# A hybrid encoder trunk on one core: the input projection with 512-column products, its halves added on eviction, a reordered opening, and short rows padded to 128

## The reference, cut to what matters

```python
u = rmsnorm(h, norm_mix[l])
proj = u @ w_in[l]
p_mla, p_ssm, p_swa = jnp.split(proj, [MLA_COLS, MLA_COLS + SSM_COLS], axis=-1)
y_a = mla_mixer(p_mla, cos, sin, ...)      # 6 heads, 128 + 64 rotary features
y_b = mamba2_mixer(p_ssm, ...)             # conv of 4 taps, SiLU, SSD scan, 12 heads
y_c = swa_mixer(p_swa, sinks, ...)         # 8 heads of 64, 2 key heads
h = h + jnp.concatenate([y_a, y_b, y_c], axis=-1) @ w_out[l]
h = h + cross_attention(rmsnorm(h, norm_cross[l]), rmsnorm(mem, norm_mem[l]), ...)
h = h + conv_ffn(rmsnorm(h, norm_ffn[l]), ...)
return rmsnorm(h, norm_final)

def causal_dwconv(x, w, b):                # in mamba2_mixer: k_w = 4
    xp = jnp.pad(x, ((0, 0), (k_w - 1, 0), (0, 0)))
    return sum(xp[:, k:k + seq] * w[k] for k in range(k_w)) + b
```

## Time and profile before

| | |
|---|---|
| median of 3 runs | 1200.29 us (1200.27 to 1201.62) |
| the profiled execution | 1203.7 us, of it 1201.8 us span |
| TensorE busy | 1180.1 us, 98% |
| VectorE busy | 893.1 us, 74% |
| ScalarE busy | 656.4 us, 55% |
| mean granted clock of TensorE | 0.994 |
| HBM | 214.33 MB read, 180 GB/s over the span |

### The profile page before, as it was taken

How to read it: one execution, slowest core, us unless ns; L and a number is a source line. 1 busy time by engine, 2 the same in 40 slices (tenths; PEclk the granted TensorE clock), 3 DMA queues, 4 the chain that set the end, 5 groups by cost and what they waited for, 6 DMA issues and landing times.

```text
span 1201.8 us, 18802 instructions
## 1 busy us (share of the span) xinstructions
PE 1180.1 (98%) x6956; PEld 1040.3 (87%) x6956; DVE 893.1 (74%) x1263; ACT 656.4 (55%) x867; POOL 0.2 (0%) x4
## 2 busy tenths in 40 slices
PE   9899999999999999999999999999999999999996
PEld 8799999988887978888888888888888888888885
DVE  5775998778776667867777777778777777777777
ACT  5545674475654557546464545455464545555454
POOL 0000000000000000000000000000000000000000
PEclk9999999999999999999999999999999999999998
DMA  9666756433566445776666657575767667585751
GB/s 351 197 165 164 194 146 176 131 107 106 188 215 185 148 142 142 222 198 191 192 177 195 188 172 209 175 209 180 204 180 204 175 185 199 172 212 175 210 175 71
DMA packets 303214, 217.11 MB, mean 181 GB/s; under 512 B 11350, under 2 KB 263998, under 8 KB 302526
## 3 DMA queue, kind: packets, MB, share of 16 engines
q1 hardware_dynamic: 302990, 216.31, 61.3%
q10 hardware_dynamic: 176, 0.14, 0.1%
HBM read 214.33 MB, written 2.10 MB: 180 GB/s over the span
## 4 chain that ended last, share of the span: by engine, by line
PE 93%; DVE 3%; ACT 2%; issue 1%; DMA 1%; SPq 0%; ACTq 0%; DVEq 0%
PE bank L1359 27%; PE bank L1363 14%; PE bank L1333 10%; PE bank L1335 10%; PE bank L1334 10%; PE bank L1336 6%; PE bank L1337 6%; PE bank L1338 6%; PE bank L1434 1%; DVE lo L780 1%; ACT hi L386 1%; PE bank L1465 1%; DMA arena<-in_mem_dram 1%; PE bank L1395 1%; PE bank L1385 0%
## 5 line engine op out<-in xcount | busy, mean ns | idle before, releaser
L780 DVE TENSOR_TENSOR lo<-raw,hi 128x2048 fp32r<-128x2048 f32 x195 | 446.5, 2290 | 126.0 <-ACT hi L386 118.4
L386 ACT CAST hi<-raw 128x2048 fp32r<-128x2048 f32 x195 | 371.8, 1912 | 99.7 <-PE bank L1335 98.6
L1359 PE MATMUL bank<-ux,hi 128*128 128x512 f32 x1408 | 336.5, 391 | 0.0
L1359 PEld LDWEIGHTS bank<-ux,hi 128*128 128x128 f32 x1408 | 259.2, 188 | 50.6 <-DVE arena L1261 0.2
L1363 PEld LDWEIGHTS bank<-ux,lo 128*128 128x128 f32 x1408 | 180.9, 191 | 7.1
L1363 PE MATMUL bank<-ux,lo 128*128 128x256 f32 x1408 | 183.1, 283 | 0.0
L1333 PE MATMUL bank<-hi,ch 128*128 128x512 f32 x464 | 181.4, 391 | 1.4 <-DVE cl L1200 1.4
L1334 PE MATMUL bank<-lo,ch 128*128 128x512 f32 x464 | 180.3, 389 | 0.0
L1335 PE MATMUL bank<-hi,cl 128*128 128x512 f32 x464 | 180.2, 388 | 0.0
L1336 PE MATMUL bank<-ux,hi 128*128 128x256 f32 (+1 forms) x592 | 171.0, 289 | 1.2 <-DVE lo L780 1.2
L1337 PE MATMUL bank<-ux,hi 128*128 128x256 f32 (+1 forms) x592 | 167.8, 283 | 0.0
(11 more groups left out here) (241 smaller groups left out, 972.8 us busy)
## 6 DMA issues: line engine op xcount, KB each, us to landing
raw<-in_ffn_w_up_dram SPq DMA_DIRECT2D x88, 1024.0 KB, 5.8
raw<-in_ffn_w_down_dram SPq DMA_DIRECT2D x44, 1024.0 KB, 5.1
raw<-in_w_in_dram SPq DMA_DIRECT2D x28, 1024.0 KB, 5.6
raw<-in_w_out_dram SPq DMA_DIRECT2D x16, 1024.0 KB, 5.2
raw<-in_cross_wkv_dram SPq DMA_DIRECT2D x7, 1024.0 KB, 9.6
arena<-in_x_dram SPq DMA_DIRECT2D x4, 1024.0 KB, 8.5
raw<-in_cross_wq_dram SPq DMA_DIRECT2D x4, 1024.0 KB, 5.4
raw<-in_cross_wo_dram SPq DMA_DIRECT2D x4, 1024.0 KB, 5.1
```

The costliest lines, as they stand in the source:

```text
L386: a.mark(act.copy(hi[:, n % RING, :], raw[:, n % RING, :]), S("hi_ready"))
L780: d.mark(dve.tensor_tensor(lo[:, n % RING, :], raw[:, n % RING, :], hi[:, n % RING, :].bitcast(F32), ALU.subtract), S("lo_ready"))
L1359: pe.matmul(bank[b][:, :], hi[:, s, k * P:(k + 1) * P], ux[:, k, :, :].rearrange("p a b -> p (a b)"), start=(k == 0), stop=False)
```

## The change

1. All 28 full tiles of w_in (8 to 13, 15 to 33 without the latent ones, 38 to 40) use `wide_product`. Its optional `mid` (other heads' work) comes between the two groups of 16. Tile 14 stays as it was.
2. Each such tile is evicted in two steps: ScalarE copies the right half of the bank to the destination (`take_low`), VectorE adds the left half to it (`sum_halves`, signal `tile_summed`). `tile_summed` frees the bank. `summed(n)` counts these signals.
3. In the convolution stage ScalarE does `conv_first(n - 1)`, `conv_low(n)`, `conv_silu(n - 1)` in turn n, and VectorE `sum_halves(n - 1)`, `split(n + 2)`, extras, `conv_rest(n - 1)`.
4. The key tile is copied into four zero-padded tiles, one for each key head and half of the partitions; the rotary key gets a second padded tile `krT_odd`; `pick`, `acum_h` and `acum_l` get 128 rows, of which 116 are zero. The clears and one copy are on VectorE, at tiles 21, 22 and 24.
5. In the opening block 2 moves ahead of the second pair of memory groups, and block 4 ahead of the squares of x.
6. In the end ScalarE scales the first two blocks of t = 0 before its squares of (1, 2), and VectorE scales the other two behind its last add. Two signals go.

The diff, with some context left out:

```diff
--- before.py
+++ after.py
@@
         yT = at(7168, 6, T)
-        swa_q, swa_k, swa_v, swa_kswap = at(8704, 4, T), at(9728, T), at(9984, T), at(10240, T)
+        swa_q, swa_v = at(8704, 4, T), at(9984, T)
+        swa_key = ((at(9728, T), at(12800, T)), (at(10240, T), at(13056, T)))
+        krT_odd = at(19968, T)
+        key_tile = at(4096, T)
         sq_swa = at(8704, 4 * T)
@@
         stat = sb("stat", [P, 2, 8])
-        pick = sb("pick", [SSM_H, SSM_H], F32R)
-        acum_h = sb("acum_h", [SSM_H, T], F32R)
-        acum_l = sb("acum_l", [SSM_H, T], F32R)
+        pick = sb("pick", [P, SSM_H], F32R)
+        acum_h = sb("acum_h", [P, T], F32R)
+        acum_l = sb("acum_l", [P, T], F32R)
         mem_r = sb("mem_r", [P, TT])
@@
                 for half in range(2):
-                    if t == 1 and half == 1:
-                        sp.wait_ge(S("out_ready_act").sem, 2)
+                    if half == t:
+                        sp.wait_ge(S("out_ready_act").sem, 2 * t + 2)
                     else:
-                        sp.wait_ge(S(f"out_ready{t}").sem, 2 * half + 2)
+                        sp.wait_ge(S(f"out_ready{t}").sem, 2)
                     cols = slice(half * 1024, (half + 1) * 1024)
@@
                                       accum_out=parts[:, t, cb:cb + 1]), S(f"final_parts{t}"))
+            def act_scale(t, cbs):
+                act.wait_ge(S("final_r").sem, t + 1)
+                act.wait_ge(S("gained").sem, 4 * t + cbs[-1] + 1)
+                for cb in cbs:
+                    c = slice(cb * 512, (cb + 1) * 512)
+                    a.mark(act.activation(hwork[:, t, c], hwork[:, t, c], ACT.Copy, scale=small[:, s_r + t:s_r + t + 1]), S("out_ready_act"))
@@
+            def take_low(n, b, dst):
+                wait_product(n)
+                a.mark(act.copy(dst, bank[b][:, T:2 * T]), S("low_taken"))
             act.dma_start(tab[:, 0:2 * P], table[:, 0:2 * P]).then_inc(S("consts_landed").sem, 16)
@@
             a.mark(act.copy(hi[:, 0, CH // 2:], raw[:, 0, CH // 2:]), S("hi_ready"))
-            for q in (1, 2, 3):
-                for g in (2 * q, 2 * q + 1):
-                    token_hi("mem", g, V_MEM, mem_bank(g))
-                split(q)
-                if q == 2:
-                    act.wait_ge(S("mem_landed3").sem, 16)
-                    a.mark(act.activation(junk, mems[:, 0, :], ACT.Square, accum_out=small[:, s_ss:s_ss + 1]), S("mem_ss"))
-                    token_root("mem")
+            for g in (2, 3):
+                token_hi("mem", g, V_MEM, mem_bank(g))
+            split(1)
+            split(2)
+            for g in (4, 5):
+                token_hi("mem", g, V_MEM, mem_bank(g))
+            act.wait_ge(S("mem_landed3").sem, 16)
+            a.mark(act.activation(junk, mems[:, 0, :], ACT.Square, accum_out=small[:, s_ss:s_ss + 1]), S("mem_ss"))
+            token_root("mem")
+            for g in (6, 7):
+                token_hi("mem", g, V_MEM, mem_bank(g))
+            split(3)
+            split(4)
             act.wait_ge(S("x_landed").sem, 32)
...
             a.mark(act.activation(xs[:, 0, :], xs[:, 0, :], ACT.Copy, scale=small[:, s_r:s_r + 1]), S("x_scaled"))
-            split(4)
             act.wait_ge(S("vecs_turned").sem, 2)
...
@@
             a.mark(act.copy(dt_rows[0:SSM_H, 0, :], b[64:64 + SSM_H, 0:T]), S("tile_taken"))
+            act.wait_ge(S("tile_summed").sem, summed(N_CQ + 5))
             squares("cq", cq_raw[:, 0:4, :], sq_cq, 4)
...
-            def conv_first(n):
+            def conv_low(n):
...
                 c = n - N_XBC
-                wait_product(n)
                 if c >= RING:
                     act.wait_ge(S("xbc_ready").sem, c - RING + 1)
-                a.mark(act.activation(convacc[:, n % RING, :], bank[n % 3][:, 0:T], ACT.Identity,
+                take_low(n, n % 3, convraw[:, n % RING, :])
+            def conv_first(n):
+                c = n - N_XBC
+                act.wait_ge(S("tile_summed").sem, summed(n))
+                a.mark(act.activation(convacc[:, n % RING, :], convraw[:, n % RING, :], ACT.Identity,
                                       scale=vecs[:, V_CW + 30 + c:V_CW + 31 + c], bias=vecs[:, V_CB + c:V_CB + c + 1]), S("conv_first"))
-                a.mark(act.copy(convraw[:, n % RING, :], bank[n % 3][:, 0:T]), S("tile_taken"))
@@
                     take_x_tok(n - 22)
-                conv_first(n)
+                if n > N_XBC:
+                    conv_first(n - 1)
+                conv_low(n)
                 if n > N_XBC:
...
                 if n == N_QKV:
+                    conv_first(n - 1)
                     conv_silu(n - 1)
@@
                 if k == 4:
-                    wait_product(n)
-                    a.mark(act.copy(swa_kswap[0:64, :], bank[n % 3][64:128, 0:T]), S("kr_parts"))
-                    a.mark(act.copy(swa_kswap[64:128, :], bank[n % 3][0:64, 0:T]), S("kr_parts"))
-                take(n, n % 3, swa_q[:, k, :] if k < 4 else (swa_k, swa_v)[k - 4])
+                    take_low(n, n % 3, key_tile)
+                    act.wait_ge(S("pads_ready").sem, 1)
+                    act.wait_ge(S("tile_summed").sem, summed(n))
+                    for g in range(2):
+                        for half in range(2):
+                            a.mark(act.copy(swa_key[g][half][64 * half:64 * half + 64, :], key_tile[64 * g:64 * g + 64, :]), S("kr_parts"))
+                else:
+                    take_low(n, n % 3, swa_q[:, k, :] if k < 4 else swa_v)
...
@@
-            a.mark(act.activation(small[:, 110:111], ones[:, 0:1], ACT.Sqrt), S("root_loaded"))
+            act.activation(small[:, 110:111], ones[:, 0:1], ACT.Sqrt)
             for t in range(TT):
                 for cb in range(4):
+                    if (t, cb) == (1, 2):
+                        act_scale(0, (0, 1))
                     last_squares(t, cb)
                 last_root(t)
-            act.wait_ge(S("final_r").sem, 2)
-            for cb in (2, 3):
-                c = slice(cb * 512, (cb + 1) * 512)
-                a.mark(act.activation(hwork[:, 1, c], hwork[:, 1, c], ACT.Copy, scale=small[:, s_r + 1:s_r + 2]), S("out_ready_act"))
+            act_scale(1, (2, 3))
@@
-            d.mark(dve.memset(warm, 0.0), S("warm_ready"))
+            d.mark(dve.memset(warm, 0.0), step)
+            def sum_halves(n):
+                if n < N_XBC:
+                    dst = cq_raw[:, n - N_CQ, :]
+                elif n < N_QKV:
+                    dst = convraw[:, n % RING, :]
+                elif n < N_ZA:
+                    dst = (swa_q[:, 0, :], swa_q[:, 1, :], swa_q[:, 2, :], swa_q[:, 3, :], key_tile, swa_v)[n - N_QKV]
+                else:
+                    dst = zT[:, n - N_ZA if n < N_U else 3 + n - N_ZB, :]
+                b = z_bank(n)
+                dve.wait_ge(S("low_taken").sem, summed(n))
+                d.mark(dve.tensor_tensor(dst, bank[b][:, 0:T], dst, ALU.add), S("tile_summed"))
             dve.wait_ge(S("vecs_ready").sem, 1)
...
@@
             for n in range(N_CQ, N_CQ + 6):
+                if n > N_CQ:
+                    sum_halves(n - 1)
                 split(n + 2)
@@
                     go(dve.tensor_scalar(sinT, sinT, tab[:, C_SGN:C_SGN + 1], None, ALU.mult))
+            sum_halves(N_CQ + 5)
             split(N_KRDT + 2)
...
                 c = n - N_XBC
-                dve.wait_ge(S("tile_taken").sem, TAKEN_XBC + c + 1)
+                dve.wait_ge(S("conv_first").sem, c + 1)
                 s = n % RING
@@
             for n in range(N_XBC, N_XBC + 10):
+                if n > N_XBC:
+                    sum_halves(n - 1)
                 split(n + 2)
@@
                 if n == 21:
-                    go(dve.tensor_copy(pick[:, :], tab[H, C_ID:C_ID + SSM_H]))
+                    for wide_ in (pick, acum_h, acum_l):
+                        d.mark(dve.memset(wide_[:, :].bitcast(F32), 0.0), step)
+                    d.settle()
+                    go(dve.tensor_copy(pick[H, :], tab[H, C_ID:C_ID + SSM_H]))
                     go(dve.tensor_copy(acum_h[H, :], acum[H, :]))
...
                     rotate(krT)
+                    go(dve.tensor_copy(krT_odd[64:128, :], krT[64:128, :]))
+                    d.mark(dve.memset(krT_odd[0:64, :], 0.0), step)
+                    d.mark(dve.memset(krT[64:128, :], 0.0), step)
                 if n == 23:
...
                     feature_scale("cq", cq_raw[:, 0:4, :], 4, rtmp_a)
-                conv_rest(n)
+                if n > N_XBC:
+                    conv_rest(n - 1)
                 if n == 24:
                     feature_scale("ckv", cq_raw[:, 4:6, :], 2, rtmp_b)
+                    for g in range(2):
+                        for half in range(2):
+                            ins = dve.memset(swa_key[g][half][64 - 64 * half:128 - 64 * half, :], 0.0)
+                            d.mark(ins, S("pads_ready") if g and half else step)
+            sum_halves(N_QKV - 1)
             split(N_QKV + 2)
```

(53 more changed lines are left out.)

62 lines of the change are left out of this document (36 added, 26 removed).

## The result

The changed kernel takes 1221.38 us (median of 4, 1220.44 to 1221.88), the kernel before 1200.95 us (median of 4; the three times known when the forecast was made had a median of 1200.29): ratio 1.0169, 95% interval 1.0155 to 1.0183. It is slower by 20.4 us. The forecast was 12.4 us slower, 1212.7 us, with a range that ended at 1220. The side was right, the time was not in the range.

What follows compares the result with a forecast made beforehand. TensorE was taken as the bound (93% of the chain). Span 1201.8 + 20.0 (convolution stall) - 7.6 (gains elsewhere) = 1214.2 us; the 12.4 put on the median 1200.29 gave 1212.7, range 1203 to 1220.

Steps and rivals of the forecast that it cites:

- Convolution stage: Tiles 15 to 24: ScalarE and VectorE wait for each other, so tile 26 starts 20.0 us late.
- turns: Tiles 17 to 24: VectorE's split to conv_rest (w), then conv_rest, SiLU and cast in series, w + 3.87 us each.
- Clears: VectorE's zeroing for the padded key tiles at tiles 21, 22 and 24: 0.25 us each, four behind the CKV scaling 1.0.
- VectorE alone is the bound: Convolution stage: SiLU's wait is covered but VectorE's queue is longer; tile 26 3.8 us late, 1196.5 us; chance 0.10.
- Restart at the low clock: Behind the long wait ahead of tile 26, TensorE restarts at the low clock, costing 1.6 us.
- The rival with 4 to 5 us: Costlier restart: two tiles after the 27 us of waiting run mostly at 1.2 GHz, 1217 us; chance 0.10.
- Spreads: SSD steps: padding 12 rows to 128 saves 0.37 us a step, 2.2 us over six.
- MLA: MLA scores padded to 128 rows: with the wide-tile saving, tiles 38 to 40 give 3.8 us, the first only 0.3.
- Sliding window: Sliding-window scores padded from 64 to 128 rows: 0.23 us lost in three of four steps, 0.7 us (0 to 1.4).
- Wide tiles: TensorE's w_in tiles: 5.57 us instead of 5.754, 0.187 us saved each, 5.2 us over 28 tiles.
- tail: End of the kernel: moving token tile 0's four scalings off VectorE's path ahead of the adds gains 0.8 us.
- Opening: Blocks 2 and 4 moved ahead of the squares remove TensorE's waits and low clock; 5.1 us gained (3 to 6).

Runs made afterwards that it cites:

- late_rest: Kernel before with only VectorE's conv_rest(n-1) moved one turn later, behind the next split and the extras; 1225.55 us.
- late_both: Kernel before with VectorE's conv_rest and ScalarE's SiLU both one turn later; 1210.24 us.
- rest24: late_both with the last conv_rest (tile 24) put back ahead of the CKV scaling; 1201.70 us.
- silu_later: Changed kernel with ScalarE's SiLU of tile n-1 moved one turn later, behind the next cast; 1205.42 us.
- silu_unpad: silu_later with the opening's block 4 where it was and sliding-window scores on 64 rows, without the four clears behind the CKV scaling; 1201.23 us.
- all_wide: Changed kernel with SiLU one turn later, sum(24) and conv_rest(24) ahead of CKV scaling, 64-row sliding-window scores, block 4's weights requested ahead of x; 1191.81 us.
- warm_stall: Changed kernel with 150 unread products of 256 columns put into TensorE's long gap before tile 26; 1218.92 us.
- pad_two: Kernel before with only the spreads and the rope half of the MLA scores padded to 128 rows; 1195.77 us.
- load_swap: Kernel before with the change's opening order, and block 4's weights requested ahead of x; 1197.34 us.
- best: Changed kernel with tiles 15 to 24, the order of the opening and the 64-row sliding-window scores as before; 1191.76 us.
- pad_swa: Kernel before with only the sliding-window scores padded to 128 rows; 1202.88 us.
- open_only: Kernel before with only the change's reordering of the opening on ScalarE and VectorE; 1202.12 us.
- conv_old: Changed kernel with the ten convolution tiles 15 to 24 done as before (narrow products, old order); 1195.51 us.
- best_swap: conv_old with 64-row sliding-window scores and block 4's weights requested ahead of x; 1188.74 us.

## Why the prediction was wrong in size

Against its own profiled execution of before the forecast was +12.4 us of span; the profiled executions differ by 1219.4 - 1201.8 = 17.6.

- **Convolution stage: right.** Forecast from tile 8 to the products ahead of tile 26: 194.7 - 64.87 = 129.8 us. Measured 130.2. late_rest showed that the order makes it, late_both and rest24 that it is two effects, turns and the place of conv_rest(24); both were terms of the sum, though the text named only the first as the mechanism. Clears were sized at 0.25 each; single ones of 256 columns took 0.27, and the four behind the CKV scaling 1.41 together instead of 1.0.
- **Rival "VectorE alone is the bound": its number was right, its name was not.** It gave 178.5 - 64.87 = 113.6 us of way with the SiLU's wait covered; silu_later has 114.5. Of the 11.3 us that TensorE waits there, 5.9 are the place of one conv_rest (late_both) and 1.4 the clears (silu_unpad); VectorE's load with the sums is some 4 us (all_wide).
- **Restart at the low clock: 1.6 forecast, 2.7 measured** (warm_stall). The 1.6 was taken from one stretch at a mean of 0.66; here the products ran at 0.50 and tile 26 at 0.77. The rival with 4 to 5 us did not come.
- **Rows: right.** Spreads 0.39 a step against 0.37. MLA: from one step to the next 10.00, 10.36 and 9.70 us in pad_two for 10.58, 11.91 and 11.26 before. That is 3.7 in all against 3.2 (the 3.8 of the sum has the saving of three wide tiles in it). The half microsecond more is the first step, which was held to gain almost nothing behind VectorE and gained 0.6. Sliding window 1.0 to 1.2 against 0.7, because all four steps pay.
- **Wide tiles and tail: right.** 5.57 us a tile. From the last product's end to the end of the span 9.2 us for 10.1, so 0.9 against 0.8.
- **Opening: this step failed.** "Gain 2.7 + 1.2 + 1.6 - 0.4 = 5.1 us (bounds 3 to 6). No DMA is in the way: block 4's load is issued as early as before and block 5's earlier." It was issued as early and needed 14.4 us, with the engines full. In the old order its cast stood behind the x squares and scaling and hid that; the step went by the issue and not by the landing. Measured gain 69.97 - 68.49 = 1.5 us, so 3.6 less; TensorE's wait grew from 2.7 to 3.9 and the low clock came behind it again. load_swap, which takes away this one wait for the weights, starts tile 8 at 63.62, ahead of the 64.87 of the forecast; 66.16 is the earliest start seen in the old order (best).
- **The frame failed too.** 12.4 was put on the median as if the execution of after would be as far above its own median as the profiled one of before was, 3.4 us. That one was long mainly in one place: its opening has the low clock twice, at 12 to 16 us and at 44 to 48 us, and the same opening with one such stretch starts tile 8 at 68.1 to 68.3 (rest24, pad_two, pad_swa). Against that, the new order gains nothing (68.5). Set against the median of 1200.95 the profiled execution of before is 2.8 us late, the one of after is not; that is the rest of the 20.4. The second stretch accounts for 1.7 of the 2.8, and for the rest 1200.95 lies between two groups of executions.

So 3.6 (opening) + 1.1 to 1.3 (restart) + 0.3 (stage) make the 5.2 from 12.4 to 17.6, and 2.8 is the step from 17.6 to 20.4.

## What to carry to other kernels

When an instruction moves one turn, write down for both engines which of the other's results it waits for and of which turn; if each needs the other's of the same turn, they add instead of overlap, and the last turn has to be worked out by itself, since long one-off work may stand between it and its reader. A cast that is moved forward needs its transfer requested before whatever it overtakes. And before a gain is counted from a wait in one profiled execution, see how far that execution stands from the median and whether its lost time is the kind that comes and goes, as low-clock stretches do.

## What the runs showed of the hardware

The 78 executions of the kernel before that ran beside the experiments fall into groups: 30 took 1200.0 to 1200.5 us, 34 took 1201.6 to 1202.1, and 14 took 1202.9 to 1204.7, with a mean granted clock of about 0.998, 0.996 and 0.994. The traces show steps of this size in the opening. Stretches of the kernel before, of pad_two and of best, which have the same order of the opening:

```profile
12.00:16.00 4.00, 4.00 (x29) 4.00 (x29) 3.55 (x6) 2.78 (x4) 0.00 (x0) 0.79 1.05 406
44.00:48.00 4.00, 4.00 (x12) 3.15 (x11) 4.00 (x6) 0.74 (x1) 0.00 (x0) 0.57 0.97 315
```

```profile
12.00:16.00 4.00, 4.00 (x36) 4.00 (x35) 3.56 (x6) 2.43 (x3) 0.00 (x0) 1.00 1.05 406
44.00:48.00 4.00, 4.00 (x14) 3.16 (x13) 3.40 (x5) 0.00 (x0) 0.00 (x0) 0.73 1.10 346
```

```profile
44.00:48.00 4.00, 4.00 (x24) 3.39 (x23) 2.91 (x4) 0.94 (x3) 0.00 (x0) 1.00 1.12 340
```

Two drops, one, none: tile 8 starts at 69.97, 68.26 and 66.16 us. The other traces with this opening fit: late_rest and late_both have both drops (69.95, 69.85), pad_swa the one at 44 us (68.22), rest24 the one at 12 us (68.11). TensorE waits 2.7 us ahead of the second place in all seven, and behind it the clock was low in five and full in two (rest24 and best). Behind a wait of 2.9 to 4.4 us there, in open_only, after, silu_later, conv_old and warm_stall, it was low each time, and so it was behind 2.7 us in silu_unpad, which has half of the new order. load_swap, all_wide and best_swap wait 0.4 us there and have no drop, and the 11 executions of load_swap lie within 0.7 us (1197.19 to 1197.87). That the groups are these drops is read from these traces; most executions have none. The Trainium skill (TensorE: Matmul & The Clock Gate, What's actually happening) says that how many products run cold differs between runs of one kernel; by that, the seven traces agree.

In the kernel after the transfer engines were full from 4 to 32 us (share 0.99 to 1.08), at 378 GB/s while block 4's 1 MB was on its way; that transfer took 14.4 us where the same size takes 5.7 us (median) for the w_in tiles. The Trainium skill (Perfetto Trace Analysis, Roofline) puts a single core's ceiling at the 16 engines' total of about 435 GB/s; by that, the trace agrees, with 364 to 413 GB/s in the stretches of 4 us between 8 and 32 us.
